# Down projections of a float32 decoder trunk by seven block products in place of eight, with the following norm taken by halves of the positions

## The reference, cut to what matters

```python
def conv_ffn(h, w_up, conv_w, conv_b, w_down):
    z = h @ w_up
    ...
    gate, up = jnp.split(z, 2, axis=-1)
    return (jax.nn.silu(gate) * up) @ w_down      # (1024 x 2816) @ (2816 x 1024)

h = h + conv_ffn(rms_norm(h, norm_ffn[layer]), ...)
# then rms_norm(h, norm_mix[1]) ahead of mixer C, or rms_norm(h, norm_final)
```

## Time and profile before

| | before |
|---|---|
| median of three runs | 2263.99 us |
| lowest, highest | 2258.77, 2264.14 us |
| the profiled execution: device time | 2264.3 us |
| the profiled execution: span of its instructions | 2262.5 us |
| mean granted TensorE clock over the span | 0.988 of full speed |
| instructions | 26,462 |

### The profile page before, as it was taken

One profiled execution on the slowest core, in us unless ns is written; L12 is line 12 of the kernel. 1 busy time (PEld: TensorE's weight loads), 2 busy tenths in 40 slices (PEclk: granted clock), 3 DMA queues, 4 the chain that ended last, 5 costly groups with the idle time before them and its releaser, 6 DMA issues.

```text
span 2262.5 us, 26462 instructions
## 1 busy us (share of the span) xinstructions
PE 2195.0 (97%) x10392; PEld 1792.5 (79%) x10392; DVE 1282.0 (57%) x1401; ACT 813.1 (36%) x1015; POOL 1152.4 (51%) x634
## 2 busy tenths in 40 slices
PE   8998999989989999999999999999899999999997
PEld 5887688768868888888888788888788888888885
DVE  5668755562776767677242413437767676772324
ACT  4221333342544444443221232025444444431313
POOL 3322211131367777777665333433777777776560
PEclk9999999999999999999999999999999999999998
DMA  4101000012322222216644111113222222166432
GB/s 158 38 29 38 29 20 20 20 30 101 112 75 84 84 84 84 84 66 241 200 141 140 59 38 38 45 40 121 75 84 84 84 84 84 66 233 209 140 126 74
DMA packets 62235, 201.49 MB, mean 89 GB/s; under 512 B 6417, under 2 KB 6690, under 8 KB 62114
## 3 DMA queue, kind: packets, MB, share of 16 engines
q1 hardware_dynamic: 60962, 195.61, 25.1%
q10 hardware_dynamic: 1152, 4.19, 0.5%
HBM read 164.13 MB, written 35.65 MB: 88 GB/s over the span
## 4 chain that ended last, share of the span: by engine, by line
PE 69%; DVE 4%; ACT 1%; POOL 1%; issue 1%; DMA 1%; ACTq 0%; SPq 0%; DVEq 0%; POOLq 0%
PE ps L1148 21%; PE ps L1110 11%; PE ps L1111 11%; PE ps L1112 11%; PE ps L718 3%; PE ps L721 3%; PE ps L724 3%; PE ps L1221 1%; PE ps L1222 1%; PE ps L1223 1%; DVE act_lo L1307 1%; PE ps L1267 1%; DMA w_raw<-w_up 0%; PE ps L1005 0%; POOL w_lo L561 0%
## 5 line engine op out<-in xcount | busy, mean ns | idle before, releaser
L515 POOL TENSOR_TENSOR w_hi<-w_raw,ones 128x1024 fp32r<-128x1024 f32 x56 | 110.7, 1977 | 626.6 <-PE ps L724 243.6
L1746 DVE TENSOR_TENSOR g_lo<-g_raw,g_hi 128x1024 fp32r<-128x1024 f32 x88 | 121.8, 1391 | 282.0 <-ACT g_hi L2134 281.9
L1110 PE MATMUL ps<-t_hi,w_hi 128*128 128x512 f32 x672 | 266.7, 397 | 14.6 <-ACT snap L2102 14.3
L1111 PE MATMUL ps<-t_lo,w_hi 128*128 128x512 f32 x672 | 264.0, 393 | 0.0
L1112 PE MATMUL ps<-t_hi,w_lo 128*128 128x512 f32 x672 | 263.9, 393 | 0.0
L561 POOL TENSOR_TENSOR w_lo<-w_raw,w_hi 128x1024 fp32r<-128x1024 f32 x84 | 156.2, 1859 | 192.1 <-ACT w_hi L2105 174.2
L561 POOL TENSOR_TENSOR w_lo<-w_sum,w_hi 128x1024 fp32r<-128x1024 f32 x84 | 228.8, 2733 | 39.2 <-ACT w_hi L2105 39.2
L1148 PE MATMUL ps<-g_hi,w_hi 128*128 128x512 f32 x704 | 221.4, 390 | 1.2 <-DVE g_lo L1746 1.2
L1148 PE MATMUL ps<-g_hi,w_lo 128*128 128x512 f32 x704 | 220.7, 389 | 0.0
L1148 PE MATMUL ps<-g_lo,w_hi 128*128 128x512 f32 x704 | 220.5, 389 | 0.0
L2134 ACT ACTIVATE g_hi<-g_raw 128x1024 fp32r<-128x1024 f32 x88 | 92.2, 1059 | 294.4 <-PE ps L1148 274.6
(11 more groups left out here) (272 smaller groups left out, 4502.1 us busy)
## 6 DMA issues: line engine op xcount, KB each, us to landing
w_raw<-w_up SPq DMA_DIRECT2D x44, 1024.0 KB, 4.9
g_raw<-g_kept SPq DMA_DIRECT2D x88, 512.0 KB, 3.6
g_kept<-gst SPq DMA_DIRECT2D x44, 512.0 KB, 2.6
w_raw<-w_dn SPq DMA_DIRECT2D x88, 256.0 KB, 4.1
w_raw<-w_in SPq DMA_DIRECT2D x24, 512.0 KB, 3.6
x_kept<-x SPq DMA_DIRECT2D x16, 512.0 KB, 8.5
x<-x_kept SPq DMA_DIRECT2D x16, 512.0 KB, 5.1
x<-xT SPq DMA_DIRECT2D x8, 512.0 KB, 8.4
```

Source lines behind the costliest of these rows:

```text
L515: pool.tensor_tensor(w_hi[:, slot, :], w_raw[:, parity, :], ones[:, 0:1].to_broadcast([P, 1024]), ALU.mult).then_inc(s_whi, 1)
L1110: pe.matmul(out, wh, bh, start=(fresh and j == 0), stop=False, skip_group_check=True)
L1111: pe.matmul(out, wh, bl, start=False, stop=False, skip_group_check=True)
L1746: dve.tensor_tensor(g_low_slot(n), g_raw[:, n % 4, :], g_hi[:, n % 6, :].bitcast(F32), ALU.subtract).then_inc(F.glo.sem, 1)
```

## The change

The down projection is now a product of 2 x 2 blocks. The weights are cut by output half (m = 0, 1) and by the parity e of the k tile, the gated tiles by that parity and by position half h. The eight block products of the plain scheme become seven (`D2, D1, D5, D6, D4, D7, D3`, in this order), each with 11 steps (one for each pair of k tiles), 77 steps t in all. A step has one 128 x 512 weight operand and one 128 x 512 operand of g side by side in one tile, and 12 matmuls of 512 columns (4 output tiles, 3 passes). The operands of D2 and D1 are raw blocks; those of D5, D6, D4, D7 and D3 are sums or differences, made by VectorE (`d_sum`). The signs that the scheme needs are put into g when it is stored: `gate` is now two instructions of 512 columns, one of them times -1.

Per step, ScalarE makes the high part of the whole tile (`d_high`, one instruction of 1024 columns, two of 512 in D6), VectorE the low part (`d_low`, the same). GpSimd has no work in the down stage any more. The raw blocks are loaded by SP in the order of `USES`, 77 entries: each is one DMA for the weight block and one for the g block (D3: weights only), 256 KB each; entries of kind 5 and 7 load two blocks more into `chain_a` or `chain_b`. From entry 12 on each load waits until the entry eight before it has been used. Entries 4 to 7 are loaded once `P4` of the last pair is done, entries from 8 on stand behind the store of the last gated tile. The x tiles are loaded back at entries 9 to 12 and 24 to 27.

Results of a product are added to x for two output tiles and one half of the positions at a time (`add`, 18 in each block). The norm behind the block is by halves of the positions: the first half's items (`item(0, i)`, i = 0 to 7) come under D3, the last product; the second half's behind it. In the last block, the final norm's first half comes under D3 likewise. The splits of the C mixer's v weights on GpSimd now follow the low parts of steps 72 to 75. The diff, cut to what matters here:

```diff
+        d_early = [sb(f"d_early{i}", 8 * i, [P, 2, HALF]) for i in range(4)]
+        d_ring = [sb(f"d_ring{i}", kb, [P, 2, HALF]) for i, kb in enumerate((44, 48, 52, 56, 168, 172, 176, 180))]
+        chain_a = sb("chain_a", 60, [P, NBLK, 2, HALF])
+        chain_b = sb("chain_b", 0, [P, NBLK, 2, HALF])
...
+        STEPS = 7 * NBLK
+        D2, D1, D5, D6, D4, D7, D3 = range(7)
+        SUM_AT = {
+            5: (6, 8, 10, 12, 14, 16, 18, 20, 22, 24, 26),
+            6: (25, 27, 28, 29, 30, 31, 32, 33, 34, 35, 37),
+            7: (13, 19, 23, 38, 40, 41, 44, 46, 48, 50, 53),
+            4: tuple(range(42, 42 + NBLK)),
+            3: tuple(range(66, 66 - NBLK, -1))}
...
+        RAW = {2: (A12, G21), 1: (A11, G11), 5: (A22, G12), 6: (A11, G22), 7: (A21, G12), 4: (A22, G21), 3: (A12, None)}
...
+        ADD_AT = (15, 16, 26, 27, 37, 39, 40, 42, 48, 50, 59, 60, 70, 71, 72, 73)
+        ITEM_AT = (67, 68, 69, 70, 73, 74, 75, 76)
+        HALF_TILES = ((0, 1, 2, 3, 4, 5, 6, 7), (4, 5, 6, 7, 0, 1, 2, 3))
...
+                def use(n):
+                    kind, k = USES[n]
+                    if kind == 5:
+                        load_w(chain_a[:, k], A21, k, F.dfa[k])
+                        load_g(chain_a[:, k], G11, k, F.dfa[k])
+                    if kind == 7:
+                        if k >= 4:
+                            sp.wait_ge(*summed(F, 7, k - 4))
+                        load_w(chain_b[:, k], A11, k, F.dfb[k % 4])
+                        load_g(chain_b[:, k], G22, k, F.dfb[k % 4])
+                    if n >= 12:
+                        was, j = USES[n - 8]
+                        if was in (2, 1, 4):
+                            sp.wait_ge(*past(F.dlo, split_count({2: D2, 1: D1, 4: D4}[was] * NBLK + j)))
+                        else:
+                            sp.wait_ge(*summed(F, was, j))
+                    w, g = RAW[kind]
+                    load_w(use_tile(n), w, k, F.draw[n % 8])
+                    if g is not None:
+                        load_g(use_tile(n), g, k, F.draw[n % 8])
+
+                def last_g(k):
+                    sp.wait_ge(*summed(F, 4, k))
+                    load_g(chain_a[:, k], G22, k, F.dfa[k])
...
                 for n in range(4):
-                    load_g(n)
-                    load_down(n)
+                    use(n)
                 keep(FT - 2)
-                for n in range(4, 6):
-                    load_g(n)
-                    load_down(n)
+                sp.wait_ge(*past(F.prod, products(FT - 1, P4)))
+                for n in range(4, 8):
+                    use(n)
                 keep(FT - 1)
-                for n in range(6, DOWN):
-                    load_g(n)
-                    load_down(n)
-                    if n == 8:
-                        sp.wait_ge(*past(F.prod, products(FT - 1, P4)))
+                for n in range(8, len(USES)):
+                    use(n)
+                    kind, k = USES[n - 8]
+                    if kind == 4:
+                        last_g(k)
+                    if n == 9:
                         for i in range(2):
                             sp.wait_ge(*past(F.kept[i], 16 * (FT // 2)))
-                    m = (n - 8) // 2
-                    if n % 2 == 0 and 0 <= m < KT:
+                    if 9 <= n < 13 or 24 <= n < 28:
+                        m = n - 9 if n < 13 else n - 20
                         sp.dma_start(x[:, m, :], x_dram[layer][m]).then_inc(s_x[m], 16)
...
-                for n in range(DOWN):
...
-                    pool.tensor_tensor(down_weight(w_hi, n), down_raw(n), ones[:, 0:1].to_broadcast([P, HALF]), ALU.mult
-                                       ).then_inc(F.dhi.sem, 1)
-                    pool.wait_ge(*past(F.dhi, n + 1))
-                    pool.tensor_tensor(down_weight(w_lo, n), down_raw(n), down_weight(w_hi, n).bitcast(F32),
-                                       ALU.subtract).then_inc(F.dlo.sem, 1)
...
-                plain(N_V + t, SLOT[t], past(f0.dk, DOWN - 6 + 2 * t))
+                plain(N_V + t, SLOT[t], past(f0.dlo, split_count(D3 * NBLK + (6, 7, 9, 8)[t])))
...
+                def down(t, m):
+                    i, s = t // NBLK, t % NBLK
+                    pe.wait_ge(*past(F.dlo, split_count(t)))
+                    w, g = d_hi[:, t % 6], d_lo[t % 6]
+                    wcols = slice(m * P, (m + 1) * P)
+                    out = ps[:, 4 * (i % 2) + m, :]
+                    pe.matmul(out, w[:, 0, wcols], w[:, 1, :], start=(s == 0 and i not in (D6, D7)), stop=False,
+                              skip_group_check=True)
+                    pe.matmul(out, w[:, 0, wcols], g[:, 1, :], start=False, stop=False, skip_group_check=True)
+                    return pe.matmul(out, g[:, 0, wcols], w[:, 1, :], start=False, stop=(s == NBLK - 1),
+                                     skip_group_check=True)
...
+                for m, ready in ((0, taken(FT - 2, C21)), (3, taken(FT - 1, C11)), (2, taken(FT - 1, C12)),
+                                 (1, taken(FT - 1, C21))):
+                    pe.wait_ge(*past(F.ev, ready))
+                    ins = down(0, m)
+                ins.then_inc(F.dk.sem, 1)
...
+                    for h, cols in enumerate(LAST):
+                        ins = dve.scalar_tensor_tensor(gst[:, p % 2, cols], fs[:, cols], (1.0, -1.0)[(h + p) % 2],
+                                                       slot2(3)[:, cols], ALU.mult, ALU.mult)
...
+                    if kind == 5:
+                        dve.wait_ge(*past(F.dfa[k], 32))
+                        ins = dve.tensor_tensor(chain_a[:, k], chain_a[:, k], raw[:], ALU.add)
...
+                        ins = dve.tensor_tensor(raw[:, 1, :], raw[:, 1, :], chain_a[:, k, 1, :], ALU.add)
...
+                    dve.tensor_tensor(lo[:], src[:], hi.bitcast(F32), ALU.subtract).then_inc(F.dlo.sem, 1)
...
+                    dve.wait_ge(*past(F.dk, NBLK * (i + 1)))
+                    bank = 4 * (i % 2) + 2 * q
+                    dve.tensor_tensor(x[:, m:m + 2, LAST[h]], x[:, m:m + 2, LAST[h]], ps[:, bank:bank + 2, :], op
...
+                for t in range(4, STEPS):
+                    for kind, k in SUMS:
+                        if SUM_AT[kind][k] == t:
+                            d_sum(kind, k)
+                    d_low(t)
+                    if t in ADD_AT:
+                        add(ADD_AT.index(t))
+                    if t in ITEM_AT:
+                        i = ITEM_AT.index(t)
+                        if last:
+                            half_accumulate(F, 0, i)
+                        else:
+                            item(0, i)
...
+                for i in range(4):
+                    item(1, i)
```

More of the change, by code:

```diff
@@ L501, in _ @@
             for h, cols in enumerate(LAST):
-                for k in range(KT):
-                    sp.wait_ge(L[h].out, k + 1)
+                for i, k in enumerate(HALF_TILES[h]):
+                    sp.wait_ge(L[h].out, i + 1)
                     sp.dma_start(outT[k][:, cols], x[:, k, cols]).then_inc(s_out, 16)
@@ L1167, in ffn @@
+                ins.then_inc(F.dk.sem, 1)
+                steps = STEPS - D_LAST if F is f1 else STEPS
+                for t in range(1, steps):
+                    i, s = t // NBLK, t % NBLK
+                    if s == 0 and i == D1:
                         pe.wait_ge(*past(F.gated, FT))
-                    for n in range(DOWN_FIRST):
-                        down(n, m, m == 3)
-                for n in range(DOWN_FIRST, FT):
+                    elif s == 0:
+                        pe.wait_ge(*past(F.xadd, sum(a[0] <= i - 2 for a in ADDS)))
@@ L1190, in ffn @@
-                for m in range(4, KT):
-                    for n in range(DOWN - DOWN_LAST, DOWN):
-                        ins = down(n, m, m == KT - 1)
-                    if m < KT - 1:
-                        ins.then_inc(F.dres.sem, 1)
+                        ins = down(t, m)
+                    ins.then_inc(F.dk.sem, 1)
+                if F is f1:
+                    for m in range(4):
+                        for t in range(steps, STEPS):
+                            ins = down(t, m)
+                        ins.then_inc(F.dres.sem, 1)
+                        if m == 0:
+                            last_sum(0)
+                    last_sum(1)
@@ L1232, in _ @@
                     v_tile(0, st, (k, k + 1))
-            pe.wait_ge(*past(f0.xadd, KT))
-            sum_squares(norms[2], slot2(3))
+            for h in range(2):
+                pe.wait_ge(*past(f0.hacc[h], KT - 1))
+            for h in range(2):
+                ins = pe.matmul(ps[:, 3 + 4 * h, :], ones[:], acc[:, LAST[h]], start=True, stop=True)
+            ins.then_inc(norms[2].sum.sem, 1)
             v_tile(0, 3)
@@ L1741, in pair @@
                     if p == FT - 1:
[L1742 to L1755 removed]
+                        d_low(2)
@@ new lines, in add @@
+                def add(n):
+                    i, m, q, h, op = ADDS[n]
```

(25 more changed lines are left out.)

374 lines of the change are left out of this document (194 added, 180 removed).

## The result

The changed kernel takes 2238.6 us (median of four runs, 2234.4 to 2240.7) against 2264.1 us before (2258.8 to 2264.9): a ratio of 0.989, interval 0.987 to 0.991. The forecast was 2231 us, in a range of 2210 to 2258. The sign came out as predicted, and so did the length of the two down stages, in part by errors that cancel; two other steps of the sum failed, and both made the kernel slower than forecast.

The account below looks back on a forecast made before the run. The prediction took the down stage to be bound by TensorE alone. Per block 30.5 - 14.1 - 1.0 - 1.5 = 13.9 us; 2264.3 - 2 x 13.9 - 5.1 = 2231 us, range 2210 to 2258.

Parts of the forecast that it names:

- Matmuls removed: Down stage: 924 matmuls in place of 1056 and no first-step wait, together 30.5 us less a block.
- Late loads: Down stage, steps 8 to 20: TensorE waits 14.1 us a block for loads at 385 GB/s.
- the 82 units: Loads of 256 KB queued from the last gated tile's store up to what step 20 needs, 21.5 MB, 55.8 us.
- The rivals of 337 and 288 GB/s: Down-stage loads held to 337 GB/s (22.1 us late, 2247 us, chance 0.15) or 288 (32.9 late, 2276 us, chance 0.08).
- that of 407 with its 11.1 us: Down-stage loads hardly late: 11.1 us at 407 GB/s, 2220 us; chance 0.20 for 2198 to 2222.
- The estimate of 2240 us by 358: Down-stage loads at the skill page's 358 GB/s: 60.0 us for the queued loads, whole kernel 2240 us.
- VectorE, 1.0 us forecast: Down stage: VectorE's added operand work makes TensorE wait 1.0 us a block (0 to 2).
- The balance of 51 us of work against 49: Down stage, steps 33 to 50: 51 us of VectorE work against 49 us of TensorE's.
- the rival of 2243 us: Steps 33 to 50: VectorE's two-input operations take 1.37 us, so VectorE is late by 6.9 us; chance 0.12.
- Slow clock, 1.5 us forecast: Down stage: two waits above 3 us each bring 1.7 us of slow clock, half hidden; 1.5 us a block.
- The v tiles, -5.1 forecast: Behind the first down stage: GpSimd's four v-weight splits done about when D3 ends, 5.1 us gained once.
- The tail, 0 forecast: Behind the last block's last matmul: the chain has the same steps, so its 17 us stay.

Follow-up runs that it names:

- e3: Changed kernel with x tiles 4 to 7 loaded behind entries 44 to 47 in place of 24 to 27; 2231.1 us.
- e7: Changed kernel with D7's first three sums moved from steps 13, 19 and 23 to 36, 38 and 39, the last ones by about a step; 2232.9 us.
- b2: b1 with D5's sums two steps later; 2205.5 us.
- b3: b2 with x tiles 0 to 3 behind entries 24 to 27 and D5's sums 5 to 8 at steps 19, 22, 23, 24; 2197.6 us.
- e9: Changed kernel with VectorE making the low parts of steps 45 to 48 twice; 2239.5 us in a single run.
- b1: Changed kernel with all x tiles and D7's first sums later, w_v loads ahead of the wait for D3's last step, and the tail reordered; 2210.5 us.
- e3b: Changed kernel with x tiles 4 to 7 behind entries 44 to 47 and 0 to 3 behind 20 to 23, two additions later; 2228.9 us.
- e1: Changed kernel with the third and fourth w_v loads issued ahead of SP's wait for D3's last step; 2233.1 us.
- e2: Changed kernel with ScalarE's and VectorE's work behind the last block in another order; 2232.2 us.

## Why the prediction was right, and where it was wrong

**Matmuls removed: right.** The pitch is 0.2267 us (60 matmuls in 13.60 us throughout the later part of the stage), 924 of them, and the first step's wait is gone. At that pitch before's first stage held 0.9 us beside its matmuls, not 0.6, so the removal is worth 30.9 us and not 30.5.

**Late loads: the mechanism right, the size 2.4 us too small.** Step 19 was forecast 12.8 us late and was 15.2; step 20's low part ended 0.4 us ahead of a TensorE that was 16.9 us late, so its operand was 16.5 late, against 14.1. The error was already there at step 10 (6.1 against 3.2), and from there to step 19 lateness grew by 9.1 us where the forecast had 9.6. The rate was right then: 391 GB/s in the full stretch, taken at 385. What was mis-sized is the start. The store was issued 8.7 us into the stage (forecast 9.0), and the forecast let the 82 units behind it have an empty link at 385 GB/s from then on. Two things were missing. The ten units of entries 4 to 7 (2.6 MB) were not all in: 238 GB/s from 1036.0 to 1045.3 make 2.2 MB, and the rest is about 1 us. And in the 9.7 us behind the store the engines moved 304 GB/s, which is 0.8 MB less than at 385 and another 2 us; the dip lies from 1049 to 1052 us, at 180 GB/s and a share of 0.74, around the 0.6 us in which SP waits for the store to land. These estimates, less the 0.3 us by which the store was early, come to about the 2.9 us by which step 10 was later than forecast. What holds the engines in the dip is open.

That the loads were the cause is shown by what their removal gives: 8 units less took 4.8 us off the 16.5 by which step 20's operand is late (e3), 8 others 5.8 (e7), so 0.60 and 0.73 us a unit where 0.681 was the price; with more of them moved, the largest lateness up to step 20 fell to 3.7 us at the wait (b2) and to nothing (b3). The rivals of 337 and 288 GB/s are out by the full stretch, and so is that of 407 with its 11.1 us. The Trainium skill (DMA: Bandwidth & Descriptors, Bandwidth) gives about 358 GB/s as a core's limit at the memory, and says that it is a core's share when both cores of a pair stream; for one core alone it has 425 in transfers of 16 MB. This kernel runs on one core, and its 384 to 392 GB/s in 50 us and more of every run lie above the one and below the other: the trace disagrees with 358 as a limit here. (The page has 358, not the 337 of the rival that names it.) The estimate of 2240 us by 358 was near the measured 2238.6 by luck, since its rate is wrong and it knew nothing of the two steps that failed. The same section's rule of 1 MiB and more per DMA, with 341 GB/s at 1 MB, does not hold for this queue either: DMAs of 256 KB, one behind another, had 387.

**VectorE, 1.0 us forecast, none measured.** The balance of 51 us of work against 49 was wrong, and not only for the lead that VectorE has built by then. VectorE's work of steps 33 to 50 took 45.05 us and 4.05 us of waiting for loads, in 49.1. The price was read from durations, and VectorE's rows overlap like TensorE's: from 1177.55 to 1178.68 are 1.13 us for an instruction that lasts 1.22, and from 1176.40 to 1177.55 are 1.15 for one of 1.23; with 512 columns, from 1179.81 to 1180.41, it is 0.60 for 0.68. By starts the same list is 46 us, so there were 3 us of room where the forecast had 2 too little. The low part ends 0.9 us ahead of TensorE's step 28, 5.3 us ahead of step 36 and 7.3 us ahead of step 47. e9 shows that even 4.9 us more cost nothing, so the rival of 2243 us is out in this kernel. In b3, where TensorE is on time, steps 33 to 50 make the first stage 1.1 us later and the second 0.1, but behind a VectorE that waited for loads; that is no sign for the 1.0.

**Slow clock, 1.5 us forecast, 0.4 measured.** Three stretches at the 1.2 GHz level stood in the first stage, not two, each worth about 1.7 us, and two of them followed waits of 2.07 and 2.06 us, where the forecast counted only waits above 3 (and wrote 1.5 for half of two times 1.7). The first two filled time that TensorE would have waited. Only the last is exposed, and step 20's operand would have been late by 16.5 without it. So a slow stretch behind a wait costs only if nothing later is late anyway: b1, b2 and e7's second stage pay the 1.7, e3b doesn't pay its longer one.

16.5 + 0.4 + 0 against 14.1 + 1.5 + 1.0, and 30.9 removed against 30.5: the stage's 13.9 us agree to 0.1 by luck, because a term 2.4 too small met two that were 2.1 too large together and a gain that was 0.4 too small.

**The v tiles, -5.1 forecast, +2.2 measured: the step that failed.** The prediction wrote that the four splits start at step 72's low part, "so all are done about when D3 ends". It looked at GpSimd's condition alone. The third and fourth w_v loads stand in SP's queue behind a wait for D3's last step, put there for two constants. For the late loads the prediction followed SP's queue; for these four it did not. e1 moves that one wait and gets 7.3 us, the forecast's 5.1 and the 2.2 together.

**The tail, 0 forecast, +3.4 measured: it failed too.** "The same steps" is true of the chain and not of what stands ahead of it on the engines. With the norm by halves the first half's variance, guess and scaling stand between the second half's items, and the last tile's addition at 2219.47 came 2.7 us after its operand. e2 reorders and has 17.2 us.

Together: -27.8 from the stages, +2.2 and +3.4 from the failed steps, -3.2 from stretches that the change hardly touches, is the -25.3 us between the spans (to 0.1, by rounding); the forecast had -32.9.

## What to carry to other kernels

When a scheme trades arithmetic for operands, write the bytes due before each step against the rate of a full link, from the moment the queue can first run: in this kernel the largest lateness in that list set the stage, and waits before it, slow clock included, cost next to nothing and gave next to nothing when removed. Then bring down the list and not the rate: sort out whatever is not due yet. Price an engine's instructions by the distance of their starts, not by their durations. And for a step moved under another, follow its loads to the queue that issues them and to every wait ahead of them there.
